# Forgetting attention in a hybrid layer: both heads of a pair walk through a query block together, value products land feature-major, low-key scores use half the contraction rows

## What is computed

```
def forgetting_attention(q, k, v, logf):      # (B, H=8, S=2048, d=64)
    F = jnp.cumsum(logf, axis=-1)
    logits = (einsum('bhqd,bhkd->bhqk', qi, k) * scale + Fi[..., :, None] - F[..., None, :])
    logits = jnp.where(kpos[None, :] <= qpos[:, None], logits, -jnp.inf)
    p = jax.nn.softmax(logits, axis=-1)
    return jnp.einsum('bhqk,bhkd->bhqd', p.astype(v.dtype), v)
...
y_f = h_f.reshape(B, S, F_W) * jax.nn.silu(f_z)
```

## Time and profile before

| | |
|---|---|
| median of 3 runs | 1825.53 us (1823.52 to 1827.44) |
| profiled execution, its own time | 1827.74 us |
| span of its trace | 1826.1 us |
| PE busy in the span | 1700.4 us, 93% |
| DVE, ACT busy | 826.4 us (45%), 490.5 us (27%) |
| mean granted TensorE clock | 0.964 |

### The profile page before, as it was taken

The page is one execution under the profiler, slowest core; times in us unless marked ns, Lnnn a source line. Parts: engine busy times, 40 slices in busy tenths (PEclk is TensorE's granted clock), DMA queues, the critical chain, the costliest instruction groups (busy, mean ns, idle before and its releaser), DMA issues. The chain is left out here.

```text
span 1826.1 us, 24542 instructions
## 1 busy us (share of the span) xinstructions
PE 1700.4 (93%) x8650; PEld 1301.9 (71%) x8650; DVE 826.4 (45%) x1819; ACT 490.5 (27%) x738; POOL 126.2 (7%) x122
## 2 busy tenths in 40 slices
PE   7689999999999999999998399999899996799998
PEld 6558888877777778888886266566565663688887
DVE  1942234221111134453111376566575664677774
ACT  1611011100010012221000255455454553322221
POOL 1610000000000000000000000000000000122221
PEclk9779999999999999999999699999999998799999
DMA  9520231321111111122111844506208101677762
GB/s 338 162 82 26 101 115 57 115 92 69 69 69 69 57 69 69 70 75 74 70 53 61 200 143 105 138 12 159 89 6 201 47 13 29 180 185 187 191 177 84
DMA packets 142094, 187.54 MB, mean 103 GB/s; under 512 B 9113, under 2 KB 116349, under 8 KB 135933
## 3 DMA queue, kind: packets, MB, share of 16 engines
q1 hardware_dynamic: 135252, 139.98, 27.8%
q0 software_dynamic: 6784, 46.89, 6.6%
HBM read 126.77 MB, written 60.06 MB: 102 GB/s over the span
## 5 line engine op out<-in xcount | busy, mean ns | idle before, releaser
L559 PE MATMUL a_ps_u<-a_h_hi,a_w_hi 128*128 128x512 f32 x1152 | 469.3, 407 | 0.0
L559 PE MATMUL a_ps_u<-a_h_lo,a_w_hi 128*128 128x512 f32 x1152 | 465.1, 404 | 0.0
L559 PE MATMUL a_ps_u<-a_h_hi,a_w_lo 128*128 128x512 f32 x1152 | 336.3, 406 | 0.0
L559 PEld LDWEIGHTS a_ps_u<-a_h_hi,a_w_hi 128*128 128x128 f32 x1152 | 216.6, 188 | 52.9 <-issue 1.9
L559 PEld LDWEIGHTS a_ps_u<-a_h_lo,a_w_hi 128*128 128x128 f32 x1152 | 216.7, 188 | 48.8
L559 PEld LDWEIGHTS a_ps_u<-a_h_hi,a_w_lo 128*128 128x128 f32 x1152 | 210.2, 188 | 51.2
L1213 DVE CUSTOM_DVE_ANT_0 f_probs<-f_ps_s,f_neg_f 128x512 f32<-128x512 f32 (+2 forms) x320 | 186.8, 608 | 130.3 <-PE f_ps_s L1101 80.4
L634 ACT ACTIVATE a_u_copy<-a_ps_u 128x2048 f32<-128x2048 f32 x28 | 52.8, 1886 | 462.9 <-PE a_ps_u L559 462.9
L1135 PE MATMUL f_ps_o<-f_probs_t,v_tok 128*64 128x512 f32 (+3 forms) x640 | 158.4, 559 | 13.4 <-ACT f_probs_t L1304 8.6
L1295 ACT ACTIVATE f_probs<-f_probs,f_neg_max 128x128 f32<-128x128 f32 (+15 forms) x128 | 153.5, 1199 | 54.5 <-DVE f_neg_max L1221 54.4
L1100 PE MATMUL f_ps_s<-k_hi,q_pack 128*128 128x512 f32 (+2 forms) x320 | 136.9, 428 | 19.3 <-DMA f_neg_f<-scratch_f_negF 13.4
(11 more groups left out here) (196 smaller groups left out, 1867.9 us busy)
## 6 DMA issues: line engine op xcount, KB each, us to landing
scratch_arrays<-a_stage POOLq DMA_DIRECT2D x27, 1024.0 KB, 4.2
a_w_land<-in_w_in SPq DMA_DIRECT2D x36, 512.0 KB, 3.8
scratch_qkT<-a_stage POOLq DMA_DIRECT2D x8, 2048.0 KB, 7.6
a_w_ring<-in_w_ada SPq DMA_DIRECT2D x12, 1024.0 KB, 9.0
a_x_ring<-in_x SPq DMA_DIRECT2D x16, 512.0 KB, 3.4
q_pack<-scratch_qkT SPq DMA_DIRECT2D x32, 256.0 KB, 7.5
k_hi<-scratch_qkT SPq DMA_DIRECT2D x32, 256.0 KB, 8.1
k_lo<-scratch_qkT SPq DMA_DIRECT2D x32, 256.0 KB, 8.6
```

The source lines that it names most:

```text
L559: ins = pe.matmul(ps_u[:, par, b, :], w[:, k, :], h[:, k, cols], start=(k == 0 and i < 2 * len(blocks) and h is h_hi), stop=(k == KT - 1 a ...
```

## The change

Both heads of a pair now go through a query block together. A step is one key tile for both heads, a block J has 4 (J + 1) steps, and while block J is worked on, the chunks of both heads of block J + 1 are dealt out by `plan`. `exp_plan` deals out the exponentials: rows whose last chunk is in a step are made in a later one.

- Value products: head h goes into partitions 64 h to 64 h + 63 of `ps_o`, all key tiles accumulate in place, and the result is feature-major at once. `fold`, `out_t`, `out_tok`, `finish` and `turn_back` are gone. In their place VectorE widens the inverse sums (`inv_wide`), TensorE transposes them (four transposes at key tile 2), VectorE multiplies them with the gate (`inv_z`) and then `ps_o` with that.
- Scores: high keys as before, one 128-row matmul for each head; the low keys lie in one tile `k_lo`, head 0 in partitions 0 to 63 and head 1 in 64 to 127, and each head's matmul uses only its 64 rows, q high times k low (the product of the low parts is left out).
- PSUM: `ps_s` is two slots of two heads, `ps_t` three banks, `ps_o` one.
- Exponentials of all eight rows of both heads are waited for at once before the first transpose of a block.
- Copies out of PSUM: ScalarE takes most of them; VectorE takes head 1 at odd key tiles in J = 1 and 2, and all of head 1 in J = 3.
- Probabilities of even blocks lie in the memory of `w_land` and a smaller tile, so the load of `w_land` moves to the last block of the last pair.

```
 def scores(n, J, m, r, c, width, last):
...
+                    for h in range(HP):
+                        pe.matmul(banks[h][:, 0:width], q_pack[:, h, rows], k_hi2[:, h, keys], start=True, stop=False)
+                    for h in range(HP):
+                        own = slice(h * F_DH, (h + 1) * F_DH)
+                        ins = pe.matmul(banks[h][:, 0:width], q_pack[own, h, rows], k_lo[own, keys],
+                                        start=False, stop=not last)
...
+                        if kt == 0 and h == 0:
+                            pe.wait_ge(exp_ready, n * N_ROWS + (J + 1) * QT * HP)
+                        taken(pe, n, u - T_BANKS)
...
+                    for h in range(HP):
+                        ins = pe.matmul(ps_o[h * F_DH:(h + 1) * F_DH, first:], v_tok[:, kt, h, :],
+                                        probs_t[:, at % 2, h, first:], start=(kt == 0), stop=(kt == key_tiles(J) - 1))
...
-                def finish(g):
-                    h, J = ORDER[g % LAST]
-                    pe.wait_ge(ot_ready, n * LAST + g + 2)
-                    for r in range(QT):
-                        rows = slice(0, F_DH if J == 0 and r == 0 else P)
-                        ins = pe.matmul(ps_o[:, r * F_DH:(r + 1) * F_DH], out_t[rows, r * P:(r + 1) * P],
-                                        fold[rows, :], start=True, stop=True)
...
+        def plan(J, last_pair):
+            n = key_tiles(J)
+            following = [] if J + 1 == GROUPS and last_pair else chunks((J + 1) % GROUPS)
+            begin, end = (n // 3, n - 3) if J + 1 == GROUPS else (0, n - 1 if J == 0 else n - 2.5)
...
+        def exp_plan(J, last_pair):
+            shares, waiting, out = plan(J, last_pair), [], []
+            for p, share in enumerate(shares):
+                left = len(shares) - 1 - p
+                count = len(waiting) if left == 0 else max(1, -(-len(waiting) // left))
+                out.append(waiting[:count])
+                waiting = waiting[count:]
+                rows = [(r, h, c * NB + width) for m, (r, c, width, last) in share if last for h in range(HP)]
+                waiting += rows
...
+                for s, (J, kt) in enumerate(STEPS):
+                    share = plan(J, last_pair)[kt]
+                    ends = kt == key_tiles(J) - 1
+                    early = len(share) if ends else (len(share) + 1) // 2
+                    where = (n, J + 1) if J + 1 < GROUPS else (n + 1, 0)
+                    for m, chunk in share[:early]:
+                        scores(*where, m, *chunk)
+                    if s + 1 < N_STEPS:
+                        turn(n, *STEPS[s + 1])
...
+                    for m, chunk in share[early:]:
+                        scores(*where, m, *chunk)
+                    product(n, J, kt)
...
-            sp.dma_start(w_land[:, :, :], a["w_out"][0].rearrange("(k p) n -> p k n", p=P)).then_inc(w_landed, 16)
...
+            sp.wait_ge(t_psum, n * len(USES) + use_at(GROUPS - 1, 0, 0))
+            sp.dma_start(w_land[:, :, :], a["w_out"][0].rearrange("(k p) n -> p k n", p=P)).then_inc(w_landed, 16)
```

More of the change, by code:

```diff
@@ L944, in forgetting_heads @@
         masks_ready = sem("masks_ready")
+        neg_f_landed = [sem(f"neg_f_landed{i}") for i in range(2)]
         s_psum = sem("s_psum")
@@ L960, in forgetting_heads @@
         w_landed = sem("w_landed")
[L964 to L970, removed]
+        assert HP == 2 and GROUPS % 2 == 0
         def chunks(J):
             return [(r, c, NB if c < J else (r + 1) * P, c == J) for r in range(QT) for c in range(J + 1)]
[L976 to L980, removed]
@@ L1001, in plan, with key_tiles @@
-        def plan(g, last):
-            n = pairs(ORDER[g][1])
-            following = [] if g + 1 == LAST and last else chunks(ORDER[(g + 1) % LAST][1])
-            steps = max(1, n - 1.5)
-            cuts = [min(len(following), math.ceil(len(following) * p / steps)) for p in range(n + 1)]
-            return [list(enumerate(following))[cuts[p]:cuts[p + 1]] for p in range(n)]
+        def key_tiles(J):
+            return QT * (J + 1)
         def columns_of(J, kt):
             return max(0, kt - QT * J) * P
+        STEPS = [(J, kt) for J in range(GROUPS) for kt in range(key_tiles(J))]
@@ L1271, in pair_of_heads @@
-                if not last_pair:
-                    odd(LAST, 0)
-                finish(LAST - 1)
-                output(LAST - 1)
+                for s, (J, kt) in enumerate(STEPS):
+                    where = (n, J + 1) if J + 1 < GROUPS else (n + 1, 0)
+                    if kt == 0 and J:
+                        output(J - 1)
+                    for m, chunk in plan(J, last_pair)[kt]:
+                        logits(*where, m, *chunk)
+                    if kt == 0:
+                        invert(J)
+                    if s + 1 < N_STEPS:
+                        copies(n, *STEPS[s + 1])
+                    elif not last_pair:
+                        copies(n + 1, 0, 0)
+                    if kt == INV_AT - 1:
+                        gate(J)
@@ L1329, in pair_of_heads @@
-                if not last_pair:
-                    even(LAST, 0)
+                for s, (J, kt) in enumerate(STEPS):
+                    where = (n, J + 1) if J + 1 < GROUPS else (n + 1, 0)
+                    ends = kt == key_tiles(J) - 1
+                    rows = exp_plan(J, last_pair)[kt]
+                    if ends:
+                        for row in rows:
+                            exponential(*where, *row)
+                    if s + 1 < N_STEPS:
+                        copies(n, *STEPS[s + 1])
+                    elif not last_pair:
+                        copies(n + 1, 0, 0)
+                    if not ends:
+                        for row in rows:
+                            exponential(*where, *row)
```

440 lines of the change are left out of this document (210 added, 230 removed).

## The result

The changed kernel takes 1883.72 us (1881.15 to 1886.34, 4 runs), the kernel before in the same comparison 1824.93 us (1823.52 to 1827.44, 4 runs): ratio 1.0321, 95% interval 1.0301 to 1.0341, so 59 us slower. The forecast was 1848, slower by 23, with a range from 1812 to 1870. The direction came out, the size didn't.

What follows compares the result with a forecast made beforehand. PE was taken as the bound; -31 us of removed work, 0 for low keys and +50 of waits made +19, plus 4 for slow matmuls: 1851, stated as 1848 us after median adjustment and rounding, range 1812 to 1870.

Steps and rivals of the forecast that it cites:

- The borders: Block starts, first transposes waiting for eight rows of two heads: 17.5 us of waits a pair, 50 us added in all.
- Rival 3: Block borders: waits half as long because VectorE and ScalarE run ahead, about 20 us and not 50, 1818; chance 0.12.
- The slow clock behind them: PE's first matmuls after waits of 5 us run slow: 4 us added for twelve borders.
- The low-key scores: 64-row low-key matmuls of both heads: overlap gains 31 us, mode changes cost 32; taken as zero.
- 160 chunks x 0.2: Low-key chunks: going from 128 rows to 64 and back costs 32 us in all.
- What the new profile would show: Signs: some 60 us of exponential waits, stage 520 us or more, wide low-key pairs 0.1 late and taking some 0.45 us.
- The fold's 0.21: Block 0's fold with 64-row matmuls, 1.07 us against 0.86 without: 0.21 us for going in and out.
- Rivals 2 and 4: Low-key matmuls: 2, halves overlap, mode change nearly free, 1817 us, chance 0.2; 4, no overlap, change paid, 1878, chance 0.08.
- The folds: Two folds for each of 16 blocks, 0.81 us of PE each: removing them gains 26 us.
- The diagonal products: Value products on the diagonal: equally wide halves take 2.76 us against 2.86, gaining 2 us over 16.
- The end of the stage: After the last product, copy, fold, multiplication and transposes become one multiplication of 0.69 us: 3 us gained once.
- Its absence at the start helps nobody that waits: Load of w_land, moved to the last pair's block 3: no gain claimed at the start from its move.

Runs made afterwards that it cites:

- e1: Changed kernel with TensorE's waits for exponentials before blocks 1, 2 and 3 filled by constant matmuls, against the changed kernel: 1852.65 us, 31 us less.
- e10: Changed kernel with waits filled and low-key matmuls over all 128 rows, against the changed kernel with filling alone: 1831.44 us, 21 less.
- e4: Kernel before with every fold done twice, against the kernel before: 1855.31 us, ratio 1.0155, 28.5 us more.

## Why the prediction was wrong, point by point

- **The borders (+50).** Right in mechanism and nearly in size. The loop's round waits 5.67 us at block 1 with 4.27 us ahead of it at the pair's start, together 9.9 (forecast 7 to 10), 5.03 at block 2 (5 to 6), 2.30 at block 3 (3 to 4): 17.3 us where 17.5 was worked out. The added idle time of the stage is 41 us by the windows; the base of "4 to 6" for a pair before was too low (28 us in four). Rival 3 is false.
- **The slow clock behind them ("I add 4 us").** The step that failed. The mechanism was named and sized as an afterthought, without a row. What filling took away measured 31 us (e1), and some 40 by the slow work in all. The trace before had the row for it. In the stage it has no wait of 5 us, but behind one of 2.46 at a pair's start eight product records took 2.98, where the earlier trace rows have 1.50:

```profile
1166.65 0.79 PE L1100 MATMUL f_ps_s<-k_hi,q_pack 128*128 128x512 f32 x1 [2.46 <-DVE f_part_max L1213]
...
1168.55 2.98 PE L1135 MATMUL f_ps_o<-f_probs_t,v_tok 128*64 128x512 f32 x8
```

  There, and at the wait of the earlier trace rows, the clock was down for 7 us, with PE busy for 5.4 and 6.1. At 0.43 lost that is 2.5 us a wait, and twelve such borders would have come to 30 and not 4.
- **The low-key scores (0, between -31 and +32).** Mis-sized: +21 (e10). That "half goes: 31 us" is the term that failed: the wide pairs gave 7 in all, 0.04 to 0.12 and not 0.24 each, since about 0.2 us of a pair is fixed, and narrow ones lost 2. "160 chunks x 0.2", 32, was too high: 0.20 in the narrow chunk shown (0.09 and 0.11), but the second part only where masks follow, 16 + 6 in all. What the new profile would show was right for this step: a wide pair that starts 0.1 late and takes some 0.45. The fold's 0.21 was a good row for it. The Trainium skill (TensorEngine Tiling (Array Packing), Key Properties) gives both halves of this, drain on a change of mode and tiles that run in parallel; the trace agrees with both (0.09 in, and 0.42 against 0.66 for a wide pair). Rivals 2 and 4 are false.
- **The folds (-26).** Right, 28.5 (e4). The diagonal products (-2): from start to start they take 0.79, 0.59 and 0.37, as worked out. The end of the stage (-3): the last products from 1597.13 and the result at 1598.84 leave no fold or copy between. Neither was tried alone.
- **"Its absence at the start helps nobody that waits."** Of `w_land` that holds. But "nine transfers" were read only for the next pair's start; the same function is called in the stage ahead, where the barrier waits for stores behind them, and gave 3.8 us there. `w_land` was asked for at 1569 us, landed in 15.5, and nothing waited for it.

The corrected sum for the stage: -28 - 2 - 3 + 21 + 41 + 31 = +60, of 64 by the windows. With the 40 of all slow work in place of 31 it would be +69, so the fit is good to some 5 us and no better. Ahead of the stage 3.8 are won, and the stages before and behind differ by some 3 between the two executions: +57.4 in span. The forecast missed by 36 us: 27 by the clock and 21 by the low keys, less 9 of added waits that were counted too high and 4 of the earlier start, is 35; that the smaller differences nearly cancel is luck.

## What to carry to other kernels

Price a TensorE wait of some us as the wait and the slow work behind it, and read the second from the granted clock of the windows behind several waits in the trace at hand; here 41 us of added idle time brought 31 more with them, and single waits of the same length between 3.7 and 15.7 us of slow work. When two engines' orders are rewritten, ask at each border what is queued behind the wait and could have been ahead of it: moving half a chunk list and one product gave 32 us without a single instruction less. And take a saving by row halves from pairs of the widths that the kernel has, and against full matmuls that stand before the same kind of instruction, since the part that doesn't shrink with the width decides.

## What the runs showed of the hardware

- After 5.67 us without work, TensorE's granted clock stayed at 0.50 through 13.3 us in which it was busy for 13.26, with transposes, products and scores mixed. Behind three other waits of that length in the same stage it came back after 3.7 to 15.7 us. In the kernel before, 2.46 and 2.67 us of waiting were followed by 7 us at 0.51. Filled with 512-column matmuls, the wait of 5.67 left it at 0.98.
- Two 64-row matmuls in different halves of the rows: 0.42 us for a pair of 512 columns, 0.31 for 256, against 0.66 for a 512-wide pair in the same half and 0.47 (before transposes) or 0.55 (before products) for two over all rows. Where they follow full-row matmuls, 0.09 is added before them, and 0.11 between the masks behind them and what follows.
- Doing the low-key matmuls one behind the other cost 59 us in the whole where their own rows give 32; the stage's mean clock was 0.85 with it and 0.88 without.
